# A two-layer decoder step on one core: one level of Strassen's scheme in the MLPs' up-projections

## The reference

```python
x = x + mix
hn = rmsnorm(x, norm_mlp[layer])
x = x + jnp.square(jax.nn.relu(hn @ w_up[layer])) @ w_down[layer]
```

## Time and profile before

| | us |
|---|---|
| median of three runs | 2369.0 |
| lowest, highest | 2367.3, 2378.8 |
| the profiled execution | 2386.2 |
| its span, first to last instruction | 2384.5 |
| first MLP | about 795 to 1181 |
| second MLP | about 1978 to 2370 |

### The profile page before, as it was taken

The page is one execution under the profiler, slowest core; times in us unless marked ns, Lnnn a source line. Parts: engine busy times, 40 slices in busy tenths (PEclk is TensorE's granted clock), DMA queues, the critical chain, the costliest instruction groups (busy, mean ns, idle before and its releaser), DMA issues.

```text
span 2384.5 us, 41895 instructions
## 1 busy us (share of the span) xinstructions
PE 2203.7 (92%) x17594; PEld 2076.8 (87%) x17594; DVE 1365.8 (57%) x2087; ACT 754.3 (32%) x1440; POOL 393.2 (16%) x267
## 2 busy tenths in 40 slices
PE   8998887898899999999998998999899879999998
PEld 7997776787789999999998988897898859999997
DVE  5786777756654535344555565664656647353444
ACT  4333334355444322122313322323332334122221
POOL 1000111001121100000035444244324500000000
PEclk9998998887999999999999999999999989999999
DMA  4225767762334787777657778468657946777774
GB/s 167 77 82 175 251 241 255 255 203 89 102 133 141 257 274 255 263 267 259 235 171 274 241 228 299 169 207 303 231 192 243 331 156 211 266 263 249 266 264 179
DMA packets 282927, 519.95 MB, mean 218 GB/s; under 512 B 17792, under 2 KB 253680, under 8 KB 278896
## 3 DMA queue, kind: packets, MB, share of 16 engines
q1 hardware_dynamic: 271424, 324.44, 41.5%
q10 hardware_dynamic: 5888, 177.91, 20.5%
q0 software_dynamic: 5440, 15.08, 1.7%
HBM read 483.76 MB, written 210.80 MB: 291 GB/s over the span
## 4 chain that ended last, share of the span: by engine, by line
PE 61%; DVE 12%; DMA 10%; issue 9%; ACT 4%; POOL 3%; SPq 1%; ACTq 0%; DVEq 0%; POOLq 0%
PE gp L2367 33%; PE gp L2948 13%; DMA uk<-in_dil_k 4%; PE gp L2520 3%; PE gp L2730 3%; DVE cacc L1611 2%; POOL uq L3054 2%; DMA decay<-tmp_a_row 2%; DMA vs<-in_dil_v 2%; PE mp L2823 1%; PE mp L2898 1%; POOL at_f L3014 1%; ACT w_hi L1032 1%; DVE sc_t L2180 1%; PE mp L2791 1%
## 5 line engine op out<-in xcount | busy, mean ns | idle before, releaser
L2948 PE MATMUL gp<-a_hi,w_hi 128*128 128x272 f32 x1152 | 350.5, 305 | 2.0 <-DVE q_t L2106 2.0
L2948 PE MATMUL gp<-a_lo,w_hi 128*128 128x272 f32 x1152 | 334.8, 292 | 0.0
L2948 PE MATMUL gp<-a_hi,w_lo 128*128 128x272 f32 x1152 | 333.6, 291 | 0.0
L2367 PE MATMUL gp<-a_hi,w_hi 128*128 128x272 f32 x1456 | 305.7, 291 | 21.1 <-DVE cin L1600 10.9
L3054 POOL TENSOR_TENSOR uq<-uq,uk 128x1024 f32<-128x1024 f32 x96 | 259.5, 2709 | 290.1 <-DMA uk<-in_dil_k 289.9
L2367 PE MATMUL gp<-a_lo,w_hi 128*128 128x272 f32 x1456 | 302.6, 289 | 0.0
L2367 PE MATMUL gp<-a_hi,w_lo 128*128 128x272 f32 x1456 | 301.7, 289 | 0.0
L2367 PEld LDWEIGHTS gp<-a_hi,w_hi 128*128 128x128 f32 x1456 | 230.8, 189 | 24.3 <-DVE cin L1600 12.6
L2948 PEld LDWEIGHTS gp<-a_hi,w_hi 128*128 128x128 f32 x1152 | 219.9, 191 | 25.7 <-issue 22.3
L2367 PEld LDWEIGHTS gp<-a_hi,w_lo 128*128 128x128 f32 x1456 | 230.2, 190 | 0.0
L2367 PEld LDWEIGHTS gp<-a_lo,w_hi 128*128 128x128 f32 x1456 | 228.7, 190 | 0.0
(11 more groups left out here) (399 smaller groups left out, 4183.2 us busy)
## 6 DMA issues: line engine op xcount, KB each, us to landing
out_dil_ks<-in_dil_k ACTq DMA_DIRECT2D x32, 2044.0 KB
out_dil_vs<-in_dil_v ACTq DMA_DIRECT2D x32, 2044.0 KB
uq<-tmp_rows SPq DMA_DIRECT2D x96, 512.0 KB, 6.5
w_raw<-in_odd_w_in SPq DMA_DIRECT2D x36, 1024.0 KB, 8.4
vs<-in_dil_v SPq DMA_DIRECT2D x67, 512.0 KB, 6.9
w_raw<-in_w_up SPq DMA_DIRECT2D x32, 1024.0 KB, 8.2
w_raw<-in_w_down SPq DMA_DIRECT2D x32, 1024.0 KB, 8.0
uk<-in_dil_k SPq DMA_DIRECT2D x64, 512.0 KB, 7.3
```

What stands on the lines that cost most here:

```text
L2367: m = nc.tensor.matmul(gp[:, c, h, 0:HALF], w[:, sl, k, c * P:(c + 1) * P], x[:, k, h * HALF:(h + 1) * HALF], start=n < 2, stop=n >= 46)
L2948: m = nc.tensor.matmul(out, w[:, k, n * P:(n + 1) * P], x[:, k, h * HALF:(h + 1) * HALF], start=k == 0 and j == 0, stop=k == last_k and j ...
```

## The change

Of each MLP's 16 up tiles the 12 with j = 1 to 3 are "fast": each is a 2 x 2 block product over halves of k (blocks of alternating k), halves of the 256 outputs and halves of the tokens, done with 7 products of 4 k-blocks x 3 passes = 12 matmuls of 128x272 in place of 8, with sums around them (Winograd's form).
- Token sums are made once an MLP, in steps m = 0 to 7: VectorE makes the normed x (x_scaled), ScalarE the rounded parts (x_high, x_high_t), GpSimd the sums (x_sums), VectorE the low parts (x_low, x_low_t), for four pairs p of k-blocks.
- Weight sums are made for every fast tile in the step before, in w_raw: VectorE low22, GpSimd two sums, low1, GpSimd two sums, low2, low3, with ScalarE's high22, high1, high2, high3.
- A fast tile m uses all four banks of gp (m even) or mp (m odd). ScalarE copies single banks out (copy_first, copy_third, copy_last), VectorE adds the others (first_sums, second_sums, last_sums). Products 5 to 7 add into banks 0, 2 and 3.
- Relu and square are one VectorE operation of 1088 columns for a tile (hidden), as are the rounding (hidden_high) and the low part (hidden_low). The token factor rstd is in the normed x for fast tiles.
- Down tiles with m mod 8 = 4 take k-blocks 6 and 7 of both chunks last.
- GpSimd's table loads go behind the first MLP. The loops over j are written out. rows_stored waits for more stores.

The core of the diff:

```diff
+def fast(m):
+    return 8 <= m < MLP_N and m % 8 < 4
+def home(m, i):
+    return (3 * (m % 8) + i) % 4
```

ScalarE:

```diff
+                def high3(m):
+                    act.wait_ge(s_sum, 1 + 4 * fast_at(lay, m) + 4)
+                    if fast(m - 1):
+                        act.wait_ge(p_mm, 1 + 5 * fast_at(lay, m) - 2)
+                    else:
+                        act.wait_ge(mm_done, chunks_before(base + m))
+                    nc.scalar.activation(w_hi_q[:, home(m, 2)], raw_unit(m % 2, 0), ACT.Copy).then_inc(w_hi_done, 1)
...
+                for m in range(MLP_N):
+                    j, u, n = m // 8, m % 8, m + 1
+                    if fast(m - 1):
+                        copy_last(m - 1)
+                    if u == 7 and fast(n):
+                        high22(n)
+                    if fast(n):
+                        high1(n)
+                    elif not fast(m):
+                        split_whole(n)
+                    if m == 0:
+                        rms(1 + 2 * lay)
+                    copy(m)
+                    if m < 8 and m % 2 == 0:
+                        x_high(m // 2)
+                    elif m < 8:
+                        x_high_t(m // 2)
+                    if m < 4:
+                        hidden_high(m)
+                    if fast(m):
+                        copy_first(m)
+                        if not fast(n):
+                            split_whole(n)
+                    if fast(n):
+                        high2(n)
+                    if fast(m):
+                        copy_third(m)
+                    if fast(n):
+                        high3(n)
+                    if fast(m - 1):
+                        hidden_high(m - 1)
+                    if fast(n) and fast(n + 1):
+                        high22(n + 1)
```

VectorE:

```diff
+                def low_unit(m, i):
+                    q = home(m, i)
+                    return nc.vector.tensor_tensor(w_lo_q[:, q], raw_unit(m % 2, i % 2), w_hi_q[:, q].bitcast(F32), ALU.subtract)
...
+                for m in range(MLP_N):
+                    j, u, n = m // 8, m % 8, m + 1
+                    if fast(n):
+                        low22(n)
+                    elif not fast(m):
+                        split_whole(n)
+                    if m == 0:
+                        inverse_rms(1 + 2 * lay)
+                    if m < 8 and m % 2 == 0:
+                        x_scaled(m // 2)
+                    if fast(m - 1):
+                        last_sums(m - 1)
+                        hidden(m - 1)
+                    if fast(n):
+                        low1(n)
+                    if m < 8 and m % 2 == 0:
+                        x_low(m // 2)
+                    elif m < 8:
+                        x_low_t(m // 2)
+                    if fast(m):
+                        first_sums(m)
+                        if not fast(n):
+                            split_whole(n)
+                    if fast(n):
+                        low2(n)
+                    if fast(m):
+                        second_sums(m)
+                    if fast(n):
+                        low3(n)
+                    if fast(m - 1):
+                        hidden_low(m - 1)
+                    if m < 4:
                         for c in range(2):
+                            drain_whole(m, c)
+                        hidden(m)
+                        hidden_low(m)
+                    elif not fast(m):
                         for c in range(2):
+                            k = 2 * u - 8 + c
+                            dve.wait_ge(mm_done, chunks_before(base + m) + c + 1)
+                            add_x(ph, 0, k)
```

TensorE (w_h, w_l, x_h and x_l are the parts of block p):

```diff
+                def times(bank, unit, odd, x, done, more=False):
+                    for p in range(4):
...
+                        for n, (w, v) in enumerate(((w_h, x_h), (w_l, x_h), (w_h, x_l))):
+                            z = nc.tensor.matmul(B[:, bank], w, v, start=p == 0 and n == 0 and not more, stop=p == 3 and n == 2,
+                                                 skip_group_check=True)
+                    z.then_inc(done, 1)
...
+                pe.wait_ge(drained, chunks_before(G - 1) if fast(m - 1) else chunks_before(G) - 1)
+                pe.wait_ge(s_lo, 3 * q + 2)
+                times(0, home(m, 0), 0, 0, p_mm)
+                times(1, home(m, 0), 1, 1, mm_done)
+                if not fast(m - 1):
+                    pe.wait_ge(drained, chunks_before(G))
+                pe.wait_ge(s_lo, 3 * q + 3)
+                times(2, home(m, 1), 1, 3, p_mm)
+                times(3, home(m, 1), 0, 4, p_mm)
+                pe.wait_ge(w_lo_done, G + 1)
+                pe.wait_ge(snap, 1 + 2 * q + 1)
+                times(0, home(m, 2), 0, 6, p_mm, True)
+                pe.wait_ge(copied_out, 4 + 3 * q + 2)
+                times(2, home(m, 2), 1, 2, p_mm, True)
+                pe.wait_ge(snap, 1 + 2 * q + 2)
+                times(3, None, 0, 5, mm_done, True)
```

GpSimd:

```diff
+                def unit_sums(m):
+                    q, s = fast_at(lay, m), m % 2
+                    a11, a12, a21, a22 = (raw_part(s, k, f) for f in range(2) for k in range(2))
+                    pool.wait_ge(s_lo, 3 * q + 1)
+                    nc.gpsimd.tensor_tensor(a22, a21, a22, ALU.add).then_inc(s_sum, 1)
+                    nc.gpsimd.tensor_tensor(a21, a11, a21, ALU.subtract).then_inc(s_sum, 1)
+                    pool.wait_ge(s_lo, 3 * q + 2)
+                    pool.wait_ge(s_sum, 1 + 4 * q + 2)
+                    nc.gpsimd.tensor_tensor(a11, a22, a11, ALU.subtract).then_inc(s_sum, 1)
+                    pool.wait_ge(s_sum, 1 + 4 * q + 3)
+                    nc.gpsimd.tensor_tensor(a12, a12, a11, ALU.subtract).then_inc(s_sum, 1)
```

More of the change, by code:

```diff
@@ L287, in turning_bank, with fast_at, parts_at, sums_at @@
     return (2 * y + h) % 3
+MLP_N = 32
+def fast(m):
+    return 8 <= m < MLP_N and m % 8 < 4
+def fast_at(lay, m):
+    return 12 * lay + 4 * (m // 8 - 1) + m % 8
+def home(m, i):
+    return (3 * (m % 8) + i) % 4
+def parts_at(lay):
+    return 4 + 4 * lay
+def sums_at(lay):
+    return 4 + 3 * lay
 def pieces():
@@ L705, in build @@
         state_done = sem("state_done")
+        s_lo = sem("s_lo")
         conv_sum = sem("conv_sum")
@@ L761, in rows_stored @@
             eng.wait_ge(v_stored[2], 64 * 4)
+            for g in range(3):
+                eng.wait_ge(k_stored[g], 16 * 4)
+            eng.wait_ge(vn_stored, 16 * 12)
             eng.wait_ge(row_stored, 16 * 24)
@@ L1377, in mlp, with copy, split_whole @@
-                turns(act, 4, body, peel_first=True, peel_last=True)
+                def copy(m):
+                    j, u = m // 8, m % 8
+                    keep(kept, 2 * j + u // 4, 511 * (u % 4), 511)
+                def split_whole(m):
+                    G = base + m
+                    if G >= G_END:
+                        return
+                    act.wait_ge(w_loaded[m % 2], 16 * (G // 2 + 1))
+                    act.wait_ge(mm_done, chunks_before(G - 1) + fast(m - 1))
+                    scale = HEAD_DIM ** -0.5 if G == G0["odd"] else 1.0
+                    nc.scalar.activation(w_hi[:, m % 2], w_raw[:, m % 2], ACT.Copy, scale=scale).then_inc(w_hi_done, 1)
@@ new lines, in low1, with low2, low3, banks @@
+                def low1(m):
+                    dve.wait_ge(s_hi, 1 + 3 * fast_at(lay, m) + 2)
+                    low_unit(m, 0).then_inc(s_lo, 1)
+                def low2(m):
+                    dve.wait_ge(s_hi, 1 + 3 * fast_at(lay, m) + 3)
+                    low_unit(m, 1).then_inc(s_lo, 1)
+                def low3(m):
+                    dve.wait_ge(w_hi_done, base + m + 1)
+                    low_unit(m, 2).then_inc(w_lo_done, 1)
+                def banks(m):
+                    return (mp if m % 2 else gb)[:, :, 0:HALF]
@@ L2770, in _ @@
+            def mlp(lay, i_norm):
+                for m in range(MLP_N):
+                    if fast(m):
+                        fast_group(lay, m)
+                    else:
+                        whole_group(lay, m, i_norm)
             mlp(0, 1)
```

283 lines of the change are left out of this document (197 added, 86 removed).

## The result

The changed kernel takes 2404.5 us (median of 4 runs, 2403.2 to 2411.4) where the kernel before takes 2369.3 on the same chip (4 runs, 2367.3 to 2378.8): ratio 1.0147, 95% interval 1.0113 to 1.018, so 35 us slower for 27 forecast. The profiled run of after took 2405.9 (span 2404.1). That of before took 2386.2, some 14 us of it lost ahead of the first MLP; so spans are not compared here, but the two MLPs, from the first of their matmuls to the last.

A forecast was written before the change was run, and what follows sets the result against it. TensorE's pace was taken to bound both MLPs. Terms -36.0 + 19.8 + 7.0 + 4 + 5.6 + 23 + 3.5 = +26.9 us, on the median of 2369.0, gave 2396 us, 1.1% slower; range 2360 to 2420.

The forecast's parts named there:

- case A: The forecast itself, all terms summed: 2396 us, own range 2384 to 2408, chance 0.58.
- rival D: Clock falls at every wait of 1 us or more, or sums take 1.4 us: 2403 to 2426; 0.12 with another rival.
- The 36.0 us saved: Both MLPs: 288 matmuls fewer at an unchanged 0.125 us each save 36.0 us.
- Wait 1: Whole tile followed by a fast one: TensorE idles 3.3 us for add_x queued behind low3, six times, 19.8 us.
- Wait 2: First tile of each MLP: token parts ahead of the first drain cost 7.0 us in sum, 4.4 without GpSimd.
- Wait 3: Token parts in steps 2 and 4: 13.0 us of work against a 12.0 us tile, 4 us in all, none without GpSimd.
- Wait 4: Down tile behind the fast ones: last activations come 0.9 us late, six times, 5.6 us; bounds 0 to 9.
- Wait 5: Inside fast tiles: GpSimd and VectorE two-input SBUF operations exclude each other, first_sums late by 1.1 and 2.7 us; 23 us.
- The clock: Two or three falls of the granted clock after long TensorE waits, 3.5 us; bounds 0 to 14.
- Tables of GpSimd at no cost: GpSimd's 17 table DMAs moved behind the first MLP land about 1.8 us before VectorE needs them, costing nothing.
- Rival B: The meeting of GpSimd and VectorE costs nothing: -2.7 us, 2366 us, no change; chance 0.22.
- rival C: VectorE's queue keeps ahead except at low3 and add_x, only six waits of 3.3 us remain: 2353 us; chance 0.08.

The follow-up runs named there:

- e9: Changed kernel with all edits of order, and VectorE instead of GpSimd making the first and third weight sum of each fast tile; 0.9890 of the kernel before.
- e12: e9 with both additions of a whole tile to x put back behind low3, as in the changed kernel; 0.9981 of the kernel before.
- e6: Changed kernel with GpSimd's four weight sums per fast tile replaced by zero fills, so its output is wrong; 1.0067 of the kernel before.
- e1: Changed kernel with both additions of a whole tile to x moved ahead of low3 of the fast tile behind it; 1.0101 of the kernel before.
- e7: Changed kernel with 24 matmuls nobody reads added at each of six fast tiles behind a whole tile, before TensorE waits; 1.0163 of the kernel before.
- e13: e12 with 24 matmuls nobody reads ahead of the wait for the drained bank at each of the six places; 0.9987 of the kernel before.

## Why the prediction was right, and where not

The forecast was 2396 us and 1.1% slower; measured were 2404.5 us and 1.5%, inside the range of 2360 to 2420, near the upper end of case A's own (2384 to 2408), where rival D begins (2403).

- **The 36.0 us saved.** Right: matmuls stay 0.125 us apart, and e9, nearly without waits, has MLPs 30.3 us shorter than before with 3.2 us of first-tile waits left.
- **Wait 1, 19.8.** Right to the step: 19.0 in after, six of up to 3.3 us, and again 19.0 in e12.
- **Wait 2, 7.0 or 4.4.** 4.3 measured, the value without GpSimd. Its sum started at 794.77, beside pa_lo, and took 1.88 us: it was the one that was held up.
- **Wait 3, 4.** None measured, for the same reason: I let GpSimd's sum get between two low parts each time. In tile 2 it starts at 819.77 and is itself held up (1.90 us), the low parts go through, and the drain comes at 820.38 right behind them.
- **Wait 4, 5.6.** 10.4 measured. The order was right, and a step called free was not: ScalarE's split of the tile after next had to wait for its weights.

```profile
921.94 7.06 SPq L1008 DMA_DIRECT2D w_raw<-in_w_down  x2
...
933.52 1.92 ACT L1414 ACTIVATE w_hi<-w_raw 128x2048 fp32r<-128x2048 f32 x1 [1.09 <-DMA w_raw<-in_w_down]
```

  The load is issued behind low3 of tile 11. With late rounds low3 comes at 920.69, 10.5 us ahead of the tile's last matmul at 931.2, and the load was in 11.6 us after its issue. In e6, with rounds on time, this idle time of ScalarE is not there.
- **Wait 5, 23.** 14.3 measured in the profile's waits (16 by the starts of the matmuls), with 0.7 and 1.7 us for my 1.1 and 2.7. The mechanism was right: e6 ends it, e9 too. The size was off since a round is 12.5 us and not 13.2. The order of its steps is the forecast's; each is a little shorter. From low22's start at 898.02, hidden ends after 3.22 us (3.24 in the forecast), low1 after 5.45 (5.72), first_sums after 5.80 (6.2), and the next low22 starts after 12.51 (13.2): an operation of VectorE starts up to 0.1 us before the one ahead ends (898.63, behind 898.02 + 0.69), where I had added handovers.
- **The clock, 3.5.** 15.2 measured: the term that was mis-sized most. I took one gap without a fall as a sign for waits of 3.3 us; by the starts of the matmuls it was 2.2 us long. In after all six waits of 3.3 us drew a fall, and some of 2 us did too; in e12 four of six. D's 34 us (a fall at every wait of 1 us) was too much: there are ten stretches for its 24 waits.
- **Tables of GpSimd at no cost.** Right: the stage between the MLPs is 797.4 us before and 797.3 after, and TensorE's wait for q_t behind the first MLP is 2.0 us in both.

With their own sizes the terms are -36.0 + 19.0 + 4.3 + 0 + 10.4 + 14.3 + 15.2 = +27.2; the starts of the matmuls find 5.4 us more idle time (53.4 for 48.0) than the profile's wait rows do, and so 32.6. Terms too high (waits 2, 3 and 5, by 15 us) and too low (wait 4 and the clock, by 16) cancel, so the nearness of 2396 to 2404.5 is in part luck. Rival B fell with e6 (w_lo 1696 and 1223 ns), rival C with waits 4 and 5, which it had at nothing. What the sum did not have at all is that its terms aren't free of one another: e1 got back 17 of 27 us, and e7 0.9 of 8.

## What to carry to other kernels

What follows is drawn from this one kernel. Fewer matmuls pay only as far as the engines that feed them keep the shorter period: add up each engine's time for one period first, with the operations that can't run at once as one engine, and then the order of the queue up to the operation wanted first. Where a two-input sum on GpSimd and VectorE's own such work share a period, the sum can be cheaper on the busier VectorE (0.69 us for 1.28), but not if it then stands ahead of what TensorE waits for. And a wait can have a price with a fall of the clock in it, which shows in full only where no later wait absorbs both.

## What the hardware showed that I had not expected

- The same idle time of 3.3 us drew a fall to 0.50 in six of six places in one kernel (after) and in four of six in another (e12); waits of 0.8 us for sq drew none in after, and of those of 1.5 to 2.2 us for b_lo one in six. A fall costs 1.5 to 1.6 us (16.9 us of 37.4 at half clock in after; 6.4 us for four in e13).
- A zero fill on GpSimd of 512 columns takes 0.53 us, and VectorE's low parts keep their 1.22 us beside it (e6), while a sum of the same columns takes 1.28 alone, up to 2.34 when it meets one, and makes a 1.22 low part 2.17 to 2.31.
- One hold-up is passed on down a chain: in e9's first tile hidden took 2.46 us for 1.29 beside a token sum. ScalarE's b_hi, b_lo, the next w_lo and the drain for which tile 2 waits stand behind it one after the other, so it can be 1.2 of the 1.6 us by which tile 2 still begins late; no run takes it away.
